# Index scores: the second product of two heads side by side in two halves of the TensorE rows, the low-by-low part left out

## The reference, cut to what matters

```python
rel = jax.nn.relu(jnp.einsum('bthd,bsd->bths', iq, ik).astype(jnp.float32))
score = jnp.einsum('bths,bth->bts', rel, iw.astype(jnp.float32))
score = jnp.where(visible[None], score, -jnp.inf)
_, sel = lax.top_k(score, topk)
```

## Time and profile before

| | |
|---|---|
| median of the runs | 2805.56 us |
| the profiled execution | 2803.79 us |
| its span in the trace | 2802.0 us |
| TensorE matmuls busy | 2679.1 us, 96% |
| VectorE busy | 2056.7 us, 73% |
| ScalarE busy | 1417.9 us, 51% |
| GpSimd busy | 1250.9 us, 45% |
| score units run | from 124.58 to 283.1 us |

### The profile page before, as it was taken

One profiled execution on the slowest core, in us unless ns is written; L12 is line 12 of the kernel. 1 busy time (PEld: TensorE's weight loads), 2 busy tenths in 40 slices (PEclk: granted clock), 3 DMA queues, 4 the chain that ended last, 5 costly groups with the idle time before them and its releaser, 6 DMA issues. The chain is left out here.

```text
span 2802.0 us, 40012 instructions
## 1 busy us (share of the span) xinstructions
PE 2679.1 (96%) x14029; PEld 2475.7 (88%) x14029; DVE 2056.7 (73%) x4123; ACT 1417.9 (51%) x2425; POOL 1250.9 (45%) x846
## 2 busy tenths in 40 slices
PE   6999999999999999999998788999989998999998
PEld 6999999999999999999998666777879997888886
DVE  6477899999999999852735578899976557555554
ACT  5377578776777778853222566777740002111111
POOL 1100288686878778783455363322253332111110
PEclk9999999999999999999999899999999999999999
DMA  4433323233433232234655532212165555122211
GB/s 170 123 117 123 126 97 119 94 123 108 131 105 122 71 138 96 91 121 136 196 158 165 152 97 73 71 50 59 49 241 160 182 172 180 49 73 74 66 57 38
DMA packets 271430, 320.35 MB, mean 114 GB/s; under 512 B 36609, under 2 KB 234753, under 8 KB 270589
## 3 DMA queue, kind: packets, MB, share of 16 engines
q1 hardware_dynamic: 170691, 189.97, 22.2%
q10 hardware_dynamic: 100538, 127.82, 13.0%
HBM read 196.36 MB, written 120.73 MB: 113 GB/s over the span
## 5 line engine op out<-in xcount | busy, mean ns | idle before, releaser
L1659 PE MATMUL psum<-hT_hi,j_whi 128*128 128x416 f32 x2440 | 870.1, 357 | 2.7 <-issue 2.6
L1659 PE MATMUL psum<-hT_hi,j_wlo 128*128 128x416 f32 x2440 | 857.4, 351 | 0.0
L1659 PE MATMUL psum<-hT_lo,j_whi 128*128 128x416 f32 x2440 | 856.4, 351 | 0.0
L1273 POOL TENSOR_TENSOR v_y<-v_y,v_product 128x422 f32<-128x422 f32 x459 | 554.1, 1247 | 87.4 <-ACT v_product L1255 87.4
L448 DVE TENSOR_SCALAR_CACHE_REDUCE s_tie<-s_key,s_bits 128x640 bf16<-128x640 f32 (+14 forms) x352 | 464.3, 1319 | 12.3
L1659 PEld LDWEIGHTS psum<-hT_hi,j_whi 128*128 128x128 f32 x2440 | 459.3, 188 | 12.2 <-issue 4.7
L1659 PEld LDWEIGHTS psum<-hT_lo,j_whi 128*128 128x128 f32 x2440 | 460.6, 189 | 9.2 <-issue 1.6
L1659 PEld LDWEIGHTS psum<-hT_hi,j_wlo 128*128 128x128 f32 x2440 | 459.2, 188 | 5.7
L1255 ACT ACTIVATE v_product<-v_x,v_taps 128x422 f32<-128x422 f32 x510 | 302.7, 641 | 86.0 <-POOL v_y L1273 57.2
L1521 ACT ACTIVATE j_out<-psum 128x416 f32<-128x416 f32 x285 | 144.5, 508 | 339.0 <-PE psum L1659 327.1
L1468 POOL TENSOR_TENSOR j_wlo<-j_w,j_whi 128x1024 fp32r<-128x1024 f32 x61 | 151.5, 2484 | 341.3 <-ACT j_whi L1503 341.2
(11 more groups left out here) (294 smaller groups left out, 4892.4 us busy)
## 6 DMA issues: line engine op xcount, KB each, us to landing
T_dram<-j_out ACTq DMA_DIRECT2D x59, 624.0 KB, 2.9
j_w<-in_w_in ACTq DMA_DIRECT2D x59, 512.0 KB, 3.8
m_gate<-T_dram SPq DMA_DIRECT2D x60, 416.0 KB, 3.5
T_dram<-j_out ACTq DMA_DIRECT2D x59, 416.0 KB, 2.4
m_oraw<-B_dram SPq DMA_DIRECT2D x15, 832.0 KB, 5.4
M_dram<-m_merged ACTq DMA_DIRECT2D x5, 1664.0 KB, 7.4
n_x<-in_x_prompt SPq DMA_DIRECT2D x16, 512.0 KB, 5.4
f_mraw<-M_dram SPq DMA_DIRECT2D x16, 512.0 KB, 4.8
```

What stands on the lines that cost most here:

```text
L1273: pool.tensor_tensor(y[k % 2][:], y[k % 2][:], product[n % RING][:], ALU.add).then_inc(added, 1)
L1659: last = pe.matmul(bank, w[p][:, k, :], h[:, k, t0:t0 + SPAN], start=(k == 0 and q == 0), stop=(k == KD - 1 and q == 2))
```

## The change

The first product of each unit stays as it is. The second one is left out for even heads at their own place. At an odd head's place both second products are issued, each with 64 rows: the even head's from partitions 0 to 63 and the odd head's from partitions 64 to 127, into two different banks. Partitions 64 to 127 of `iqs` hold the low part, so VectorE writes a further tensor `iq_odd`, which has the high part of the two odd heads there. The low-by-low part is no longer computed.

```diff
+    iq_odd = [ib(f"i_iqodd{p}", [P, IH // 2, P], F32R) for p in range(2)]
...
             pe.matmul(c.psum[:, 5 + n % 3, 0:w], iqs[i % 2][:, h, :], hi[:, a:a + w], start=True, stop=False)
-            pe.matmul(c.psum[:, 5 + n % 3, 0:w], iqs[i % 2][:, h, :], lo[:, a:a + w], start=False, stop=True).then_inc(product, 1)
+            if h % 2:
+                even, odd = c.psum[:, 5 + (n - 1) % 3, 0:w], c.psum[:, 5 + n % 3, 0:w]
+                pe.matmul(even, iqs[i % 2][0:HD, h - 1, :], lo[0:HD, a:a + w], start=False, stop=True).then_inc(product, 1)
+                pe.matmul(odd, iq_odd[i % 2][HD:P, h // 2, :], lo[HD:P, a:a + w], start=False, stop=True).then_inc(product, 1)
...
             steps.did_wait(vec.tensor_copy(iqs[p][:], iq2[p][:]))
+            steps.did_wait(vec.tensor_copy(iq_odd[p][HD:P], iq2[p][HD:P, 1::2, :]))
             vec.tensor_tensor(iqs[p][HD:P], iq2[p][HD:P], f32(iqs[p][HD:P]), ALU.subtract).then_inc(iqs_ready, 1)
```

## The result

The changed kernel takes 2823.24 us (median of five runs, 2821.69 to 2824.15) against 2805.56 us of the kernel before: 17.7 us or 0.63% slower, ratio 1.0064 with a 95% interval of 1.005 to 1.0077. Forecast were 2830 us and a range of 2819 to 2842. The sign and the range hold; the likeliest case (A) was 7 us too slow, and rival C, put at 2821, is nearest to what happened.

The account below looks back on a forecast made before the run. TensorE's matmul stream was taken to bound the score stretch. Row changes 31.2 us, plus late second loads 9.0, less 16.3 saved, gave +23.9; with 1 us of waits, 2830 us, range 2819 to 2842.

Parts of the forecast that it names:

- the likeliest case (A): Score second products run side by side, the second weight load 0.11 us late: 2830 us, chance 0.48.
- rival C: Score second products run side by side at once, the second load hidden too: +15.5 us, 2821 us, chance 0.14.
- What bounds: In the score stretch TensorE's matmul stream is busy 158.6 of 158.8 us; gains or losses pass whole to the end.
- Every later stage as long as before: Behind the scores, every stage was to keep its length; only the score stretch grows, to some 183 us from 158.8.
- The four losses: TensorE going from 128 to 64 rows and back: 0.38 us per pair of heads, 82 times, 31.2 us.
- What side by side can give back: One second product's time saved per pair of heads in the scores, at most 16.3 us over 82 pairs.
- How much of it comes back: At each pair the second half streams 0.11 us after the first, 9.0 us over 82 pairs.
- B: Score second products not side by side, both halves streaming one after the other: +32 us, 2838 us, chance 0.26.
- Waits for `relu`: TensorE waiting in the scores, chiefly where a job begins, as products come later: 1 us, bounds 0 and 4.
- The cast on VectorE: 15 casts of 64 x 256 for the extra tensor, 0.2 to 0.7 us each, costed at nothing, at most 10 us.
- E, the gain: Half-array weights load ahead across the switch, losses vanish, 16.3 us saved: 2789 us, chance 0.06.
- S: Price of one matmul in TensorE's dense stream, 0.45 ns a column: 0.13 us at 288 columns, 0.23 at 512.

Follow-up runs that it names:

- full-row kernel: Changed kernel with both second products still at the odd head's place, but using all 128 rows (low by low included): 2809.39 us, 1.0015 of the kernel before.
- burst of eight: Against the kernel before, a projection span's eight score units run in one burst as 64-row side-by-side pairs: 2809.45 us with 6 banks, 2802.20 with 7.
- six banks: Kernel before with a span's eight score units in one burst of 64-row pairs, using banks 5, 6, 7 and three free projection banks: 2809.45 us.
- three pairs at the odd head: Changed kernel with all three products of both heads run at the odd head's place as side-by-side pairs of 64 rows: 2821.70 us.

## Why the prediction was right, and where it was off

- **What bounds** (TensorE in the stretch, everything passed on): right. Of the 20.4 us between the two profiled executions 16.8 are in the stretch, and they reach the end. "Every later stage as long as before" holds for the next 1162 us; behind them 3.4 us were added that the prediction didn't have and no run explains.
- **The four losses**, 0.38 us, bounds 0.35 to 0.43, from transposes of 34 rows and matmuls of 32: right. Two experiments measured 0.387 and 0.385 us for matmuls of 64 rows, and the losses around one pair of the changed kernel add up to 0.40.
- **What side by side can give back**, at most 16.3 us: right in kind; 14.9 were measured (31.7 - 16.8).
- **How much of it comes back**: the term of the sum that was mis-sized. It was put at 9.0 us and is next to nothing (0.00 or 0.01 us per pair). The prediction took the second half to stream 0.11 us behind the first, 9.0 us in all, since two loads behind a drain stand 0.11 us apart in the earlier trace rows. Those two loads go to the same rows. In the changed kernel, with different halves, the distance is 0.01 us; with both in one half it is 0.11 again. The row was read rightly, but it was applied to a case that it doesn't cover; the prediction itself noted under B that those two share their rows. Case C, which left this term out, gave +15.5 us for a measured 17.7. The forecast of 2830 lay 7 us off for this reason, and the range held because it reached down to C. What the Trainium skill says in "TensorE: Matmul & The Clock Gate", Part 3, that packed matmuls start about 4 ns apart, speaks for C, and the records here agree with it within their 0.01 us. C had been given a chance of 0.14.
- **Waits for `relu`**, 1 us, bounds 0 and 4: right. In the changed kernel the load stream waits 1.8 us for ScalarE where it was 1.0; in the full-row kernel 3.0.
- **The cast on VectorE**, taken as hidden: right, by the run with the cast alone. It took 0.29 us, in the bounds.
- **E, the gain**: excluded, since the losses per pair (0.39 us) are above S (0.13 to 0.23) in every pair. The prediction gave a condition for it, losses per pair below S. The burst of eight meets it in another way: the losses don't vanish, but four pairs of heads share one, 0.10 us each.

## What to carry to other kernels

Matmuls in two halves of the array's rows do run for the price of one here (the run with both in one half lost 14.9 us more), but going from full rows to half rows and back costs a fixed time, 0.39 us, as much as one and a half to three of the matmuls saved. Count the changes, not the matmuls. Each pair of heads saves one matmul. With one pair of heads per change the kernel loses (+16.8 us in the stretch), with two it about breaks even (-0.5), with four it gains (-6.7), if there are PSUM banks enough that the burst doesn't wait for its readers (+1.0 with six banks). A gain in one stage must also be followed to the end: most of the 6.7 us showed in the time only when a load 250 us later was issued earlier. A distance read from a trace holds for the operands it was read from: ask whether the two records shared a resource that the new ones don't.

## What had not been expected of the hardware

- Behind full-row matmuls, two weight loads of 64 rows to different halves start within 0.01 us of each other (82 pairs of the changed kernel), two to the same half 0.10 or 0.11 us apart (82 pairs with both in one half).
- Inside a run of 64-row pairs only the first step loses, 0.10 to 0.11 us; from then on a step takes 0.23 us at 512 columns, as with full rows, while each does the work of two heads (three pairs at the odd head). A wait inside the run brings that loss back: 0.28 us for the step behind it at 384 columns, where 0.175 is usual (six banks).
